# Packing the state-space mixer's small matmuls four tiles at a time in a two-layer decoder kernel

## What is computed

```python
bu = jnp.einsum('bsgh,gph->bsgp', uf.astype(jnp.complex64), b_bar)
_, states = lax.associative_scan(combine, (a, bu), axis=1)
y = jnp.einsum('bsgp,ghp->bsgh', states, c_mat).real + d_skip * uf
```

## Time and profile before

| | |
|---|---|
| runs | 1259.84, 1260.60, 1260.87 us |
| profiled execution | 1260.28 us, its span 1258.4 us, PE clock 1.00 of 2.4 GHz |
| busy | PE 1236.4 us (98%), DVE 903.7 (72%), ACT 636.4 (51%), POOL 334.7 (27%) |
| small S5 matmuls | 64 records in, 64 records out, mean 400 and 385 ns |
| idle time of PE | 14.1 us at the start, 2.8 us "issue", 1.4 us other |

### The profile page before, as it was taken

One profiled execution on the slowest core, in us unless ns is written; L12 is line 12 of the kernel. 1 busy time (PEld: TensorE's weight loads), 2 busy tenths in 40 slices (PEclk: granted clock), 3 DMA queues, 4 the chain that ended last, 5 costly groups with the idle time before them and its releaser, 6 DMA issues.

```text
span 1258.4 us, 25593 instructions
## 1 busy us (share of the span) xinstructions
PE 1236.4 (98%) x10328; PEld 1214.7 (97%) x10328; DVE 903.7 (72%) x1168; ACT 636.4 (51%) x900; POOL 334.7 (27%) x462
## 2 busy tenths in 40 slices
PE   5999999999999999999999999999999999999998
PEld 5999999999999999999999999999999999999998
DVE  4757857889887875555676577588997788655654
ACT  5645445683553453444456445458635445443442
POOL 0288900344303300000005896003443041000000
PEclk9999999999999999999999999999999999999999
DMA  7545554543344555555445545554434455555551
GB/s 306 195 173 182 185 200 145 191 168 126 114 165 168 196 216 197 181 185 198 169 145 197 194 167 200 175 184 162 150 120 147 154 184 201 173 196 184 183 171 63
DMA packets 31029, 220.46 MB, mean 175 GB/s; under 512 B 3568, under 2 KB 3568, under 8 KB 4592
## 3 DMA queue, kind: packets, MB, share of 16 engines
q1 hardware_dynamic: 30960, 219.49, 50.3%
HBM read 218.42 MB, written 1.05 MB: 174 GB/s over the span
## 4 chain that ended last, share of the span: by engine, by line
PE 96%; DVE 2%; ACT 0%; issue 0%; DMA 0%; SPq 0%; DVEq 0%; ACTq 0%
PE banks L456 31%; PE banks L457 30%; PE banks L458 30%; PE banks L469 5%; DVE w_lo_t L1085 1%; DVE u_lo_t L1099 1%; DVE hT L1238 1%; DMA hT<-x_t 0%; PE banks L663 0%; PE banks L706 0%; DVE sbqk L1182 0%; ACT L863 0%; ACT L838 0%; ACT u_hi_t L838 0%; ACT w_hi_t L825 0%
## 5 line engine op out<-in xcount | busy, mean ns | idle before, releaser
L1085 DVE TENSOR_TENSOR w_lo_t<-raw,w_hi_t 128x1024 fp32r<-128x1024 f32 x404 | 517.7, 1321 | 106.0 <-ACT w_hi_t L825 105.8
L825 ACT ACTIVATE w_hi_t<-raw 128x1024 fp32r<-128x1024 f32 x404 | 403.5, 1046 | 119.7 <-PE banks L458 119.2
L456 PE MATMUL banks<-u_hi_t,w_hi_t 128*128 128x256 f32 x1520 | 435.3, 286 | 14.5 <-DVE w_lo_t L1085 14.1
L457 PE MATMUL banks<-u_lo_t,w_hi_t 128*128 128x256 f32 x1520 | 430.9, 283 | 0.0
L458 PE MATMUL banks<-u_hi_t,w_lo_t 128*128 128x256 f32 x1520 | 430.8, 283 | 0.0
L456 PEld LDWEIGHTS banks<-u_hi_t,w_hi_t 128*128 128x128 f32 x1520 | 292.4, 192 | 20.9 <-DVE w_lo_t L1085 14.1
L457 PEld LDWEIGHTS banks<-u_lo_t,w_hi_t 128*128 128x128 f32 x1520 | 292.6, 192 | 0.1
L458 PEld LDWEIGHTS banks<-u_hi_t,w_lo_t 128*128 128x128 f32 x1520 | 292.4, 192 | 0.0
L456 PE MATMUL banks<-b_hi_t,w_hi_t 128*128 128x256 f32 x864 | 244.8, 283 | 0.0
L457 PE MATMUL banks<-b_lo_t,w_hi_t 128*128 128x256 f32 x864 | 244.5, 283 | 0.0
L458 PE MATMUL banks<-b_hi_t,w_lo_t 128*128 128x256 f32 x864 | 244.5, 283 | 0.0
(11 more groups left out here) (215 smaller groups left out, 1271.0 us busy)
## 6 DMA issues: line engine op xcount, KB each, us to landing
raw<-weights SPq DMA_DIRECT2D x203, 1024.0 KB, 4.9
prm<-params SPq DMA_DIRECT2D x1, 1178.5 KB, 5.1
prm<-params SPq DMA_DIRECT2D x1, 1166.5 KB, 14.8
cst<-constants SPq DMA_DIRECT2D x1, 1027.0 KB, 10.9
hT<-x_t SPq DMA_DIRECT2D x2, 512.0 KB, 5.6
raw<-weights SPq DMA_DIRECT2D x2, 512.0 KB, 6.4
out_t<-hT SPq DMA_DIRECT2D x4, 256.0 KB, 2.2
prm<-params SPq DMA_DIRECT2D x1, 12.0 KB, 1.8
```

Source lines behind the costliest of these rows:

```text
L456: pe.matmul(o, st[0], mv[0], start=start, stop=False, skip_group_check=True)
L457: pe.matmul(o, st[0], mv[1], start=False, stop=False, skip_group_check=True)
L825: act.activation(w_hi[:, slot, a:a + HALF], raw[:, slot, a:a + HALF], ACT.Copy) \
L1085: dve.tensor_tensor(w_lo[:, slot, a:a + HALF], raw[:, slot, a:a + HALF], w_hi[:, slot, a:a + HALF].bitcast(F32), ALU.subtract) \
```

## The change

The eight inputs become three blocks instead of four: pairs 0 and 1 go together at step 1, in four row groups, pair 1 into banks 4 and 5. The outputs become two blocks instead of four: tiles 0 to 3 at step 10 and 4 to 7 at step 18, in four column groups of bank 3. Pair 1 is rotated and scanned in `G[:, 0]` (`s5x_early`), the states of pair 0 go to `attB`, those of pair 2 to `G[:, 1, 4:8]`. DVE's `s5_rotate` is split: four products at step 1, four additions at step 2, eight scans at step 3; pairs 2 and 3 stay at steps 9 and 13. POOL no longer waits for PE between pairs 0, 1 and 2. New waits: `sb_scores(0)` and `(1)` for the second rotation (they use banks 4 and 5); DVE's evacuation of gate block (0, 0) at step 7, and ACT's square into `ropeX` at step 7, for the states of pairs 0 and 1 (`s5_state` 4), since both write `G[:, 0]`.

```diff
+S5_IN = {1: (0, 1), 9: (2,), 13: (3,)}
+S5_OUT = {10: 0, 18: 1}
 
...
         rotC, rotS = G[:, 2, :, :], G[:, 3, :, :]
+        s5x_early = G[:, 0, :, :].rearrange("p (a b c) t -> p a b c t", a=2, b=2)
+        s5x_of = [s5x, s5x_early, s5x, s5x]
+        st_early = attB[:, :, :].rearrange("p h c -> p (h c)")[:, 0:4 * T].rearrange("p (a b t) -> p a b t", a=2, b=2)
+        st_late = G[:, 1, 4:8, :].rearrange("p (a b) t -> p a b t", a=2)
+        st_of = [st_early, st, st_late, st]
         squares = [U[:, 2 * q:2 * q + 2, :] for q in range(4)]
         ab, hf = sbqk, yb[:, :, 0, :]
...
                             ins = single(o[:, P:T], v[:, 1, 64 * h:64 * h + 64], att[:, h, T:ATT], False, True)
                         return ins
 
-                    def s5_in(pair):
-
+                    def s5_in(pairs):
+
+                        pair = pairs[0]
                         if pair == 0:
                             pe.wait_ge(s.evac_v, layer * PER.evac_v + NTH[SLOT["s5u"]])
                         else:
...
                         if pair == 3:
                             pe.wait_ge(s.gla_attm, layer * PER.gla_attm + HEADS)
                         for part in range(2):
-                            for i in (2 * pair, 2 * pair + 1):
+                            for i in range(2 * pair, 2 * pair + 2 * len(pairs)):
                                 q = 32 * (i % 4)
                                 a = PARAM["s5_b"][0] + (part * 2 + i // 4) * P
-                                ins = single(banks[:, 6 + i % 2, part * T:(part + 1) * T], prm[q:q + 32, a:a + P],
+                                bank = (4 if i // 2 == 1 else 6) + i % 2
+                                ins = single(banks[:, bank, part * T:(part + 1) * T], prm[q:q + 32, a:a + P],
                                              s5u[q:q + 32, i // 4, :], part == 0, True)
                         ins.then_inc(s.s5_p, 1)
 
-                    def s5_out(pair):
-
-                        pe.wait_ge(s.s5_state, layer * PER.s5_state + 2 * pair + 2)
-                        if pair == 0:
+                    def s5_out(half):
+
+                        pe.wait_ge(s.s5_state, layer * PER.s5_state + 4 * half + 4)
+                        if half == 0:
                             pe.wait_ge(s.s5_coef, layer * PER.s5_coef + 1)
                         for part in range(2):
-                            for i in (2 * pair, 2 * pair + 1):
+                            for i in range(4 * half, 4 * half + 4):
                                 q = 32 * (i % 4)
-                                o = banks[q:q + 32, 3, (i // 4) * T:(i // 4 + 1) * T]
-                                ins = single(o, s5c[:, part, i, :], st[:, i % 2, part, :], part == 0 and i < 4, part == 1)
+                                o = banks[q:q + 32, 3, half * T:(half + 1) * T]
+                                ins = single(o, s5c[:, part, i, :], st_of[i // 2][:, i % 2, part, :],
+                                             part == 0 and half == 0, part == 1)
                         ins.then_inc(s.s5_y, 1)
 
                     def sb_scores(h):
                         pe.wait_ge(s.evac_v, layer * PER.evac_v + NTH[SLOT["sbk"]])
+                        if h < 2:
+                            pe.wait_ge(s.s5_rot, layer * PER.s5_rot + 2)
                         if h >= 2:
                             pe.wait_ge(s.sb_exp, layer * PER.sb_exp + h - 1)
                         scores(4 + h % 2, sbk, sbq, h).then_inc(s.sb_z, 1)
...
                         ins.then_inc(s.dsa_pt, 1)
 
                     def pieces(m):
-                        if m in S5_AT:
-                            s5_in(S5_AT.index(m))
-                        if m - 5 in S5_AT:
-                            s5_out(S5_AT.index(m - 5))
+                        if m in S5_IN:
+                            s5_in(S5_IN[m])
+                        if m in S5_OUT:
+                            s5_out(S5_OUT[m])
                         if m == 3:
                             sb_scores(0), sb_scores(1)
                         if m == 4:
...
                         act.wait_ge(s.evac_a, layer * PER.evac_a + NTH[SLOT["dk"]])
+                        act.wait_ge(s.s5_state, layer * PER.s5_state + 4)
                         act.activation(ropeX, dqk[:, :, :, :], ACT.Square).then_inc(s.dsa_sq, 1)
                     if m == 9:
                         act.wait_ge(s.dsa_ms, layer * PER.dsa_ms + 1)
...
                     add_squares(layer * 3 + (1 if f == 0 else 3))
                     rest_of_weights(layer, k0 + i + 1, 2)
 
-                def s5_rotate(pair):
-
-                    dve.wait_ge(s.s5_p, layer * PER.s5_p + pair + 1)
+                def s5_times(pair):
+
+                    dve.wait_ge(s.s5_p, layer * PER.s5_p + max(1, pair))
                     if pair == 0:
                         dve.wait_ge(s.s5_tab, layer * PER.s5_tab + 1)
-                    else:
+                    if pair >= 2:
                         dve.wait_ge(s.s5_state, layer * PER.s5_state + 2 * pair)
-                    i = 2 * pair
-                    bank = banks[:, 6:8, :].rearrange("p i (c t) -> p i c t", c=2)
-                    wide = lambda x: x[:, i:i + 2, :].unsqueeze(2).to_broadcast([P, 2, 2, T])
-                    dve.tensor_tensor(s5x[:, :, 0, :, :], bank, wide(rotC), ALU.mult)
-                    dve.tensor_tensor(s5x[:, :, 1, :, :], bank, wide(rotS), ALU.mult).then_inc(s.s5_rot, 1)
+                    i, x = 2 * pair, s5x_of[pair]
+                    bank = banks[:, 4:6, :] if pair == 1 else banks[:, 6:8, :]
+                    bank = bank.rearrange("p i (c t) -> p i c t", c=2)
+                    wide = lambda r: r[:, i:i + 2, :].unsqueeze(2).to_broadcast([P, 2, 2, T])
+                    dve.tensor_tensor(x[:, :, 0, :, :], bank, wide(rotC), ALU.mult)
+                    dve.tensor_tensor(x[:, :, 1, :, :], bank, wide(rotS), ALU.mult).then_inc(s.s5_rot, 1)
+
+                def s5_add(pair):
                     dve.wait_ge(s.s5_rot, layer * PER.s5_rot + pair + 1)
-                    re, im = s5x[:, :, 0, 0, :], s5x[:, :, 0, 1, :]
-                    dve.tensor_tensor(re, re, s5x[:, :, 1, 1, :], ALU.add)
-                    dve.tensor_tensor(im, im, s5x[:, :, 1, 0, :], ALU.subtract).then_inc(s.s5_x, 1)
+                    x = s5x_of[pair]
+                    re, im = x[:, :, 0, 0, :], x[:, :, 0, 1, :]
+                    dve.tensor_tensor(re, re, x[:, :, 1, 1, :], ALU.add)
+                    dve.tensor_tensor(im, im, x[:, :, 1, 0, :], ALU.subtract).then_inc(s.s5_x, 1)
 
                 def s5_scan(pair):
                     dve.wait_ge(s.s5_x, layer * PER.s5_x + pair + 1)
+                    x = s5x_of[pair]
                     for i in (2 * pair, 2 * pair + 1):
                         decay = s5n[:, 2, i:i + 1].to_broadcast([P, T])
                         for part in range(2):
-                            ins = dve.tensor_tensor_scan(s5x[:, i % 2, 1, part, :], decay, s5x[:, i % 2, 0, part, :],
+                            ins = dve.tensor_tensor_scan(x[:, i % 2, 1, part, :], decay, x[:, i % 2, 0, part, :],
                                                          0.0, ALU.mult, ALU.add)
                     ins.then_inc(s.s5_scan, 1)
 
...
                         branch_lo(1, 3, yb[:, 0, :, :].rearrange("p a t -> p (a t)"), 0.25)
-                    if m in S5_AT:
-                        s5_rotate(S5_AT.index(m))
-                    if m - 1 in S5_AT:
-                        s5_scan(S5_AT.index(m - 1))
+                    if m == 1:
+                        s5_times(0), s5_times(1)
+                    if m == 2:
+                        s5_add(0), s5_add(1)
+                    if m == 3:
+                        s5_scan(0), s5_scan(1)
+                    if m in (9, 13):
+                        pair = S5_IN[m][0]
+                        s5_times(pair), s5_add(pair)
+                    if m in (10, 14):
+                        s5_scan(S5_IN[m - 1][0])
 
                 def gate(dt):
...
                                 gate(2 * q + 1)
                             continue
+                        if SEQ[m] == (0, 0):
+                            dve.wait_ge(s.s5_state, layer * PER.s5_state + 4)
                         if not BY_ACT[m]:
                             evacuate(m)
                         rest_of_weights(layer, k0 + m // RING + 1, m % RING)
...
                     pool.tensor_tensor(s5c[:, 1, :, :], s5c[:, 1, :, :], t, ALU.add).then_inc(s.s5_coef, 1)
 
                 def s5_pair(pair):
-                    x = s5x
+                    x, y = s5x_of[pair], st_of[pair]
                     pool.wait_ge(s.s5_scan, layer * PER.s5_scan + pair + 1)
-                    if pair >= 1:
-                        pool.wait_ge(s.s5_y, layer * PER.s5_y + pair)
+                    if pair == 3:
+                        pool.wait_ge(s.s5_y, layer * PER.s5_y + 1)
                     for i in range(2):
```

(11 more changed lines are left out.)

## The result

The changed kernel takes **1265.84 us** (median of 5 runs, 1265.09 to 1267.43) where the kernel before took 1260.6 (median of 5 beside it): the ratio of the means is 1.0047, with a 95% interval of 1.0032 to 1.0061. It is slower, by 5.2 us between the medians. The forecast was 1261.8 and no change, its range ended at 1265.5.

What follows compares the result with a forecast made beforehand. PE, holding 96% of the chain, was taken to bound the kernel. Per layer 1.3 + 0.4 - 0.99 = +0.7 us, doubled on 1260.28 gives 1261.7, 1262.0 on the median's scale; forecast 1261.8, range 1255.0 to 1265.5.

Steps and rivals of the forecast that it cites:

- What PE sheds: Input block of step 5, output blocks of steps 6 and 14 go: 3.43 us a layer, 6.86 in all; double blocks last no longer.
- the column groups' rival: Four column groups go two by two: 0.86 us more at steps 10 and 18 in each layer, 1265.2 us; chance 0.12.
- the half saving: Scans take no turns with POOL, or it meets fewer halves; PE waits 1.6 us at step 7: 1256.9 to 1258.7; chance 0.20.
- DVE and POOL up to the scans: Pair 1's work moves ahead on DVE: POOL starts at 241.4, 5.4 us late; second four scans take 3.9 us beside it.
- Step 7, the softplus: DVE's first softplus result comes at 260.5 to 261.0, so PE, at `sb_suffix` by 257.6, waits some 3.1 us.
- Step 8, the exp: States ready at 267.2 delay evacuation, tanh and exp; `sb_scores(2)` starts at 268.95, PE waits 0.65 us more.
- step 12: At the attend product, without slack, PE loses 0 to 0.9 us more a layer; 0.4 taken.
- my case: The forecast itself: +0.7 us a layer (-0.1 to +1.4), 1261.8 us, no change that can be told; chance 0.50.
- The square on ACT: ACT's square at step 7 waits for the same states as the evacuation; nobody waits for it until step 9.
- the full saving: DVE's and POOL's delays stay hidden, all of PE's removed work counts: 1253.4 us; chance 0.08.
- a later POOL: Short DVE instructions take turns too, states 4 come at 269 or later; at 268.5 it is 1264.4 us; chance 0.10.

Runs made afterwards that it cites:

- e3: Changed kernel with seven useless fp32 products on PE ahead of `sb_scores(2)`, filling the wait there: 1264.47 us.
- e1: Changed kernel, with the gate block's evacuation at step 7 waiting for three states in place of four: 1263.78 us, ratio 1.0029 to the kernel before.
- e5: On top of e1, ACT's square of step 7 goes into the idle `yb` and waits for no state: 1256.26 us, ratio 0.9969 to the kernel before.
- e7: e5 plus softplus 0 to 3 and `sb_w` 2 and 3 ahead of `w_lo` halves, and ACT's step 14 copy and square ahead of the tanh: 1253.63 us.
- e9_square_alone: Changed kernel with the square in `yb` without its wait; the gate's evacuation still waits for four states: 1265.95 us, ratio 1.0048 to the kernel before.

## Why the prediction was wrong

- **What PE sheds**: right. 1.27 and 1.19 us for the double blocks; the column groups' rival is out. The estimate from the Trainium skill, "TensorE: Matmul & The Clock Gate", section "Measured speedup vs the span model", was 0.23 us more a block; the trace has 0.01, and the measurement decides. The middle of the half saving, 1256.9 to 1258.7, should have read 1257.8 and not 1257.3; nothing hangs on it.
- **DVE and POOL up to the scans**: right. POOL started at 241.18 (241.4), and the second four scans took 3.91 us (3.9), the three beside POOL 1.16 each and the one ahead of it 0.67. Scans take turns with POOL, which no row before could show.
- **Step 7, the softplus**: wrong by over two us. The first result was there at 258.23, not 260.5 to 261.0. The four halves of steps 4 and 5 took 6.26 for my 6.7, the gate steps 2.7 for 3.9, and the halves of step 6 2.9. I had let three POOL instructions in among the five gate steps, 2.1 us; it was 0.8. Their scan took 1.11 beside 0.69 alone and the step behind it 0.53 beside 0.17, the others hardly waited. So PE waited 0.69, not 3.1.
- **Step 8, the exp**: the states were ready at 267.28 (267.2) and the block started at 269.20 (268.95). But since PE hadn't waited at step 7 it stood there from 266.2 on, and the wait that I put at 0.65 was 2.98. The sum of the two waits, 3.67, is what I had (3.75); its place was not. That the sum held is no luck: the exp alone sets when PE passes step 8, and POOL met the six halves much as I had counted them.
- **The step that failed** is the price of such a wait. I counted its idle time and nothing behind it. The runs show in its place that either wait cost 0.4 us more than its idle time, and that the long one had the slow clock behind it. That clock, 1.5 us a layer, is in no term and no rival of mine, though I had forecast a wait of 3.1 us at step 7, longer than the 2.98 that brought it here. My layer was +0.7. Against the layer's start the exp came 0.47 later than I had it, the overlap that builds up again at step 8 costs 0.35, the clock 1.48; step 12 took 0.4 less, steps 15 and 17 0.3 more. That makes the 2.9 measured. Without the clock term it would have been +1.4, the upper end of my case, 1263.1 by the profile. The kernel that kept its clock, e3, took 1264.47, since part of the gain came back at step 15: inside my range, but 2.7 us over the forecast.
- **The square on ACT**: I wrote that nobody waits for it until step 9. DVE reads it at step 8 already (L1359), without idle time; what counts is the work queued behind it on ACT. In the changed kernel it cost nothing, but e1 shows that it was the next thing to hold PE, at 3.8 us a layer (7.5 between e1 and e5).

The rivals: the full saving was out of reach here and is reached in e7 (1253.6; I had 1253.4 for it). The scans that take no turns, the column groups and a later POOL are refuted by their rows. The time ended on the slower side by none of them.

What stays open: why the longer runs of the changed kernel (1267.3 and 1267.4) have a clock of 0.996 where the others have 0.997; their traces weren't taken. Open is also what lengthens steps 15 and 17 of the changed kernel by 0.3 us.

## What to carry to other kernels

Where one engine is busy 98% of the time and others feed it just in time, work taken from it turns into waiting unless the producers come earlier too. Look for what stands between a product that is waited for and its engine's queue (here, weight halves with slack), and move both together. A new wait in an in-order queue is priced by what stands behind it, buffer reuse by the part of the buffer that is really overwritten; two waits for the same event are to be repaired together before either is judged. And an idle stretch of TensorE of some us is not priced by its length: look at the granted clock behind it.

## What the runs showed of the hardware

- Four column groups of 32 run as two do: 16 records in 1.19 us, 8 in 1.18.
- A scan of 128x256 fp32 beside POOL takes 1.16 us and not 0.67, and POOL's instruction beside scans about 1.1, where beside `w_lo` halves it takes 1.7.
- A wait of PE costs about 0.4 us more than its idle time: 1.14 for 0.69, 3.39 for 2.98.
- Behind 2.98 us of idleness the granted clock was 0.51 for about 3.4 us, beginning 1.7 us after PE had started again (0.9 us in layer 1; 1.2 and 0.2 in the trace of e9_square_alone, which has the same waits). The kernel whose profile shows 2.6 us had a mean clock of 0.996 in two of five runs and 1.000 in three. A stretch filled with useless products kept it at 1.00.
